# Weight chunks of a mixture-of-experts layer loaded in runs of four instead of two

## The chip, the cores and the metric

The kernel runs on one core of a Trainium2 chip. The metric is the device time of one execution in microseconds (us). All arithmetic is in float32, with float32r (a reduced form) for one scatter product.

## The reference

One layer of a streaming encoder for 256 prompt rows and 64 sample rows of width 1024. First a mixer: RMS norm, one input projection, sliding-window attention with sinks, a short convolution, an output projection and the residual. Then a mixture of experts, in which nearly all of the weight bytes lie:

```
logits = hn @ w_router + b_router                # 32 experts
top 4 per row, gates = softmax of the four logits
for each expert e, on the rows that chose it:
    g, u = split(x @ w_gu[e] + b_gu[e])          # w_gu[e]: 1024 x 2048
    g = min(g, 7);  u = clip(u, -7, 7)
    y = ((u + 1) * g * sigmoid(1.702 * g)) @ w_down[e] + b_down[e]   # 1024 x 1024
h += gate * y, put back to its rows
```

w_gu is 32 x 8 MB and w_down is 32 x 4 MB, 384 MB in all (MB is 2^20 bytes here, KB 2^10), and each expert's weights are read once.

## The kernel before

**Tiling.** 32 experts are worked in 16 pairs. An expert's weights are 12 chunks of 1 MB, each 8 KB on each of 128 partitions: chunks 0 to 7 hold w_gu (one tile k of 128 input features each) and chunks 8 to 11 hold w_down. The two experts of a pair share TensorE: the even one uses 64 columns of the array, the odd one the other 64, and their matmuls run side by side (L854 and L856 for gate and up, L870 and L872 for down). So a step of TensorE needs the same chunk of both experts.

**Order of TensorE's work.** `pair(j)` (L933) does the eight steps k = 0 to 7 of pair j's gate and up, and then the four down steps m = 0 to 3 of pair j - 1. Between the steps stand smaller pieces: after k = 1, 3 and 5 the scatter of pair j - 2 back to its rows (L896, two half tiles each time), after k = 3 and 5 a gather of the rows of pair j + 1 (L787), and after m = 0 the turn of pair j's gate and up results by transposes (L881) and of the one-hot marks (L888). `gate_up` (L849) and `down` (L863) wait for their two chunks (`landed`, L845) and add 1 to `chunk_used` for each chunk when its last matmul is done. IN_USE (L316) lists all 384 chunks in this order, even and odd in turn; `used_up_to(e, c)` is a chunk's place in it.

**The ring.** Chunks land in a ring of 16 slots of 1 MB (L109 to L124). Three chunks have rooms of their own (EARLY_AT, LATE_AT, PIECES_AT); the other 381 go round the ring in the order of ORDER, chunk n in slot (n + 1) mod 16. LOADS (L339) says which neighbours in ORDER come by one DMA: from n = 24 (EARLY) on, two chunks of one expert at a time, 2 MB; the first 24 and the last 36 (FINE) singly. For that ORDER takes two chunks of the even expert, then the same two of the odd one. In DRAM the weights are read so that a partition holds neighbouring rows: 16 KB a partition for two chunks (`gu_dram`, `dn_dram`, L311 and L312).

**Issue.** SyncE issues every load, in order, from one queue (L462 to L464). Before each load it waits until `chunk_used` shows that TensorE is done with what lay in all of the load's slots 16 places earlier in ORDER; a load of several chunks waits for the last of these. The chunks of the first ring turn are issued while the mixer still runs, as its weights leave their rooms (L437 to L456).

**Which row is where.** Since a partition holds neighbouring rows of the weights, the features of x and of the hidden rows are picked with the same stride: `tile_features` (L376) for the gather's columns of hn, `features` (L370) for the columns of gu_sb that the transposes take, and the biases b_guT and the norm's gain g2 are loaded in that order (L443, L527).

Of the kernel before, what the change touches and what calls it, by code (L numbers as in the profile page):

```python
# [15 lines left out]
P = 128  # L16
# [13 lines left out]
def hybrid_layer_kernel(nc, x_prompt, x_sample, cache_k, cache_v, state_conv, norm1_g, w_in, q_norm_g,  # L30
# [15 lines left out]
    FF = w_down.shape[2]  # L46
    KT = D // P
    FT = FF // P
# [12 lines left out]
    FLAT = 2 * FF  # L61
    GUC, DNC = KT, FT * D // FLAT
    CH = GUC + DNC
    FPC = FLAT // D
    RING = 16
# [5 lines left out]
    with ctx:  # L71
# [111 lines left out]
        g2 = sb("g2", [P, KT])  # L183
        b_guT = sb("b_guT", [P, NE, 2 * FT])
# [123 lines left out]

        ADDED_LATE = 2 * NT * (PAIRS - 2) - 2 * NT

        gu_dram = w_gu.rearrange("l e (m p a) f -> (l e) m p (a f)", a=2, p=P)  # L311
        dn_dram = w_down.rearrange("l e (m p a) n -> (l e) m p (a n)", a=2 * FPC, p=P)  # L312

        IN_USE, ORDER = [], []  # L316
        for j in range(PAIRS + 1):
            for pair, chunks in ((j, range(GUC)), (j - 1, range(GUC, CH))):
                if 0 <= pair < PAIRS:
                    IN_USE += [(2 * pair + s, c) for c in chunks for s in range(2)]  # L320
                    ORDER += [(2 * pair + s, c + a) for c in chunks[::2] for s in range(2) for a in range(2)]
        ALL = len(IN_USE)

        EARLY, FINE = 3 * GUC, 4 * GUC + 4
        ORDER[:EARLY] = IN_USE[:EARLY]
        ORDER[ALL - FINE:] = IN_USE[ALL - FINE:]
        EARLY_AT, LATE_AT, PIECES_AT = (1, CH - 1), (NE - 2, 0), (NE - 4, 0)
        for at in (EARLY_AT, LATE_AT, PIECES_AT):
            ORDER.remove(at)
        RINGED = len(ORDER)  # L330
# [2 lines left out]
        def slot_of(n):  # L333
            return (n + 1) % RING
# [3 lines left out]

        LOADS, n = [], 0  # L339
        while n < RINGED - 2:  # L340
            e, c = ORDER[n]
            two = (EARLY <= n < RINGED + 1 - FINE and c % 2 == 0 and ORDER[n + 1] == (e, c + 1)
                   and slot_of(n) < RING - 1)
            LOADS.append((n, 1 + two))
            n += 1 + two

        def quarters(chunk):
            return [chunk[:, n * 512:(n + 1) * 512] for n in range(FLAT // 512)]
# [14 lines left out]
        def key_window(c):  # L363
# [3 lines left out]
            first = max(0, c - WIN // CHUNK)  # L367
            return (first % 2) * CHUNK, (c + 1 - first) * CHUNK

        def features(part, f):  # L370
            m, a = f // (2 * FPC), f % (2 * FPC)
            first = part * FF + m * 2 * FPC * P + a
            return slice(first, first + 2 * FPC * (P - 1) + 1, 2 * FPC)


        def tile_features(k):  # L376
            first = k // 2 * 2 * P + k % 2
            return slice(first, first + 2 * P - 1, 2)

        def most_rows(eng):  # L380
            eng.wait_ge(counts_ready, 2)
# [26 lines left out]
        @block.sync  # L408
        def _(sp):
            def rows_of(e, c, many):  # L410
                src = gu_dram[e, c // 2] if c < GUC else dn_dram[e, (c - GUC) // 2]
                return src[:, c % 2 * FLAT:(c % 2 + many) * FLAT]

            def load(e, c, many, slot):
                sp.dma_start(ring[:, slot:slot + many, :].rearrange("p a n -> p (a n)"),
# [21 lines left out]
            for n in range(RING - 1):  # L437
                slot = slot_of(n)
                if slot == FREE_SLOTS:
                    sp.wait_ge(v_done, 1)  # L440
                if slot == QKV_SLOTS:

                    for q in range(2 * FF // (4 * P)):  # L443
                        sp.dma_start(b_guT[:, :, 4 * q:4 * q + 4],
                                     b_gu[0].rearrange("e (q p a) -> q p e a", p=P, a=4)[q]).then_inc(bias_in, 16)
                    sp.wait_ge(bch_done, 3 * CT)
                if slot == BCH_SLOTS:
                    sp.wait_ge(att_mixed, NCH)
                    sp.wait_ge(conv_mixed, CT)
                    sp.dma_start(early_chunk[:, :], rows_of(*EARLY_AT, 1)).then_inc(early_in, 16)  # L450
                if BCH_SLOTS <= slot < BCH_SLOTS + MIX // 2 - 1:
                    sp.wait_ge(wo_used, slot - BCH_SLOTS + 1)
                if slot == BCH_SLOTS + MIX // 2 - 1:
                    sp.wait_ge(out_done, 2 * NT)
                    sp.wait_ge(u_kept, 2)
                load(*ORDER[n], 1, slot)  # L456
# [46 lines left out]
        @block.gpsimd  # L503
        def _(pool):
            pool.memset(ident[:, :], 0.0).then_inc(zeroed, 1)
            pool.memset(ones[:, :], 1.0).then_inc(zeroed, 1)
            pool.wait_ge(zeroed, 2)
            pool.affine_select(out=ident[:, :], in_=ident[:, :], compare_op=ALU.not_equal, fill=1.0,
                               base=0, pattern=[[-1, P]], channel_multiplier=1).then_inc(consts, 1)

            pool.affine_select(out=before[:, :], in_=ones[:, :], compare_op=ALU.is_gt, fill=0.0,
                               base=0, pattern=[[1, P]], channel_multiplier=-1).then_inc(consts, 1)
            pool.iota(row_ids[:, :], pattern=[[1, CAP]], base=1, channel_multiplier=0,
                      allow_small_or_imprecise_dtypes=True).then_inc(consts, 1)
            pool.wait_ge(consts, 3)
            pool.memset(hn[DEC:P, NT - 1, :], 0.0).then_inc(hn_padded, 1)


            roll = WIN - DEC
            rows_of = lambda a: a[0, 0].rearrange("t h d -> t (h d)")  # L520
            pool.wait_ge(ck_in, 16)
            pool.dma_start(rows_of(new_k_sample)[0:roll, :], ck_nat[DEC:WIN, :]).then_inc(kv_stored, 16)
            pool.wait_ge(cv_in, 16)
            pool.dma_start(rows_of(new_v_sample)[0:roll, :], cv_nat[DEC:WIN, :]).then_inc(kv_stored, 16)
            pool.wait_ge(v_ready, 2)
            pool.dma_start(w_rt[:, :, :], w_router.rearrange("l (k p) e -> p (l k) e", p=P)).then_inc(router_in, 16)
            pool.dma_start(g2[:, :].rearrange("p (m a) -> p m a", a=2),  # L527
                           norm2_g.rearrange("l (m p a) -> p (l m) a", a=2, p=P)).then_inc(router_in, 16)
            pool.dma_start(b_rt[:, :], b_router.to_broadcast([P, NE])).then_inc(router_in, 16)
            pool.dma_start(rows_of(new_v_prompt), v_nat[:, 1, :]).then_inc(kv_stored, 16)  # L530
            pool.dma_start(rows_of(new_v_sample)[roll:WIN, :], v_nat[0:DEC, 2, :]).then_inc(kv_stored, 16)
            pool.wait_ge(k_out_ready, 2)
            pool.dma_start(rows_of(new_k_prompt), k_out[:, 0, :]).then_inc(kv_stored, 16)
            pool.dma_start(rows_of(new_k_sample)[roll:WIN, :], k_out[0:DEC, 1, :]).then_inc(kv_stored, 16)
            pool.wait_ge(chunk_used, used_up_to(*PIECES_AT))
            pool.dma_start(b_dn[:, :], b_down[0]).then_inc(b_down_in, 16)
# [779 lines left out]
        def _(dve):  # L1316
# [309 lines left out]
            for j in range(PAIRS):  # L1626
                if 1 <= j < PAIRS - 1:
                    dve.wait_ge(gathered, 2 * (j + 1))
                    mark(2 * j + 2).then_inc(oh_ready, 1)
                if j == 0:  # L1630
                    finish_routing()
                if j == 1:
                    dve.wait_ge(bias_in, 4 * 16)
                    gate_and_up(1, gu_banks(0), 0)
                if j >= 1:
                    if j >= 2:
                        dve.wait_ge(chunk_used, used_up_to(2 * j - 3, CH - 1))
                    hidden(j, j - 1)
                if j >= 2:
                    dve.wait_ge(gate_ready, j - 1)  # L1640
                    dve.wait_ge(scattered, 2 * NT * (j - 2))
                    split_yl(j - 1, Y)
                for u in range(2 * NT):
                    if j >= 2:
                        add_rows(2 * NT * (j - 2), u, u % 2)
                    if u in (3, 5) and j + 1 < PAIRS:
                        if j >= 1:
                            dve.wait_ge(he_ready, j)
                        copy_xT(j + 2, j + 1, (u - 3) // 2)
                if j >= 1:  # L1650
                    if j >= 2:
                        dve.wait_ge(oh_turned, j - 1)
                    mark_gates(j, 2 * j - 2)
                dve.wait_ge(chunk_used, used_up_to(2 * j + 1, GUC - 1))
                if j >= 1:
                    dve.wait_ge(he_ready, j)
                copy_u(gu_banks(j))
                if j >= 1:
                    gate_and_up(j + 1, gu_banks(j), 2 * j)
                    dve.wait_ge(scattered, 2 * NT * (j - 1))  # L1660
                    if j >= 2:
                        dve.wait_ge(yl_ready, j - 1)
                        dve.wait_ge(yh_ready, j - 1)
                    split_ohT(j, ohT)
# [85 lines left out]
```

## Time and profile before

| | us |
|---|---|
| median of 3 runs (lowest to highest) | 1076.94 (1076.07 to 1077.82) |
| the profiled execution's own time | 1075.5 |
| its span in the profile | 1073.6 |
| TensorE matmuls busy | 1029.4 (96%) |
| VectorE busy | 317.7 (30%) |
| ScalarE busy | 95.7 (9%) |
| share of the chain that ended last: TensorE, DMA | 68%, 30% |
| moved by DMA over the span | 420.31 MB (10^6), mean 391 GB/s |
| granted TensorE clock, mean | 0.989 of 2.4 GHz |

The profile shows one execution. Its page sums each engine's busy time, cuts the span into 40 equal slices, follows the chain of work that ended last, and groups instructions by line. Idle time of an engine is put down to what released it. The end of a matmul is modelled, so TensorE's starts are read here rather than its busy share.

### The profile page before, as it was taken

The numbers are of one execution on the slowest core, as the hardware profiler recorded it, in microseconds if no ns is written. First come the engines' busy times: TensorE is split into PE (matmuls) and PEld (weight loads), VectorE is DVE, ScalarE is ACT, GpSimd is POOL, SyncE is SP. The second block draws the span as 40 slices with busy tenths as digits, with TensorE's granted clock in tenths as the row PEclk, the third lists the DMA queues.
The fourth block names the chain that finished last, engine by engine and source line by source line (L and its number), as shares of the span: only waits on it lengthen the run. The fifth ranks groups of instructions, "written<-read, shape, count | busy, mean of one in ns | idle before, by whom it ended". The sixth has DMA issues, their size and how long they took to land.

```text
span 1073.6 us, 11705 instructions
## 1 busy us (share of the span) xinstructions
PE 1029.4 (96%) x5101; PEld 491.1 (46%) x5102; DVE 317.7 (30%) x491; ACT 95.7 (9%) x163; POOL 8.3 (1%) x20
## 2 busy tenths in 40 slices
PE   9999999999999999989898989989898989999997
PEld 7767454444444443435353534434353435334333
DVE  3533121332323232322313231323223132313243
ACT  2222130100000000000001010000000010100001
POOL 1100000000000000000000000000000000000000
PEclk9999999999999999999999999989999999999999
DMA  9950779999999999999999999999999999999996
GB/s 356 312 118 1 258 279 408 427 427 427 426 428 427 429 428 429 429 429 426 429 429 429 429 429 430 428 427 429 428 429 429 429 430 428 427 418 418 422 421 263
DMA packets 58543, 420.31 MB, mean 391 GB/s; under 512 B 23045, under 2 KB 23345, under 8 KB 29969
## 3 DMA queue, kind: packets, MB, share of 16 engines
q1 hardware_dynamic: 55840, 419.32, 94.6%
q0 software_dynamic: 352, 0.55, 0.2%
q8 instruction: 21, 0.34, 0.1%
q10 hardware_dynamic: 2320, 0.03, 0.1%
q14 instruction: 10, 0.07, 0.0%
HBM read 418.29 MB, written 1.58 MB: 391 GB/s over the span
## 4 chain that ended last, share of the span: by engine, by line
PE 68%; DMA 30%; issue 0%; SPq 0%; DVE 0%; ACT 0%; DVEq 0%
PE ps L854 35%; DMA ring<-in_w_gu_dram 28%; PE ps L787 7%; PE ps L870 6%; PE ps L709 5%; PE ps L896 3%; PE ps L727 3%; DMA ring<-in_w_down_dram 2%; PE ps L585 2%; PE ps L856 1%; PE ps L881 1%; PE ps L738 1%; PE ps L900 1%; PE ps L1024 1%; PE ps L611 1%; PE ps L677 0%
## 5 line engine op out<-in xcount | busy, mean ns | idle before, releaser
L854 PE MATMUL ps<-ring,xT 128*64 128x512 f32 x1008 | 457.3, 607 | 31.5 <-DMA ring<-in_w_gu_dram 31.3
L856 PE MATMUL ps<-ring,xT 128*64 128x512 f32 x1024 | 464.7, 607 | 0.0
L854 PEld LDWEIGHTS ps<-ring,xT 128*64 128x64 f32 x1008 | 135.6, 139 | 306.4 <-issue 301.9
L870 PE MATMUL ps<-ring,he 128*64 128x512 f32 x480 | 213.5, 594 | 3.4 <-DMA ring<-in_w_down_dram 2.5
L872 PE MATMUL ps<-ring,he 128*64 128x512 f32 x472 | 210.5, 596 | 0.0
L1613 DVE TENSOR_TENSOR x<-ps,x 128x512 f32<-128x512 f32 (+1 forms) x84 | 54.3, 683 | 297.8 <-PE ps L896 271.8
L856 PEld LDWEIGHTS ps<-ring,xT 128*64 128x64 f32 x1024 | 137.6, 139 | 0.0
L870 PEld LDWEIGHTS ps<-ring,he 128*64 128x64 f32 x480 | 63.1, 137 | 133.6 <-issue 133.6
L787 PEld LDWEIGHTS ps<-oh,hn 128*128 128x128 f32 x720 | 89.5, 196 | 8.3 <-issue 6.0
L787 PE MATMUL ps<-oh,hn 128*128 128x128 f32 x720 | 91.5, 282 | 0.0
L1256 ACT COPY gu_sb<-ps 128x1024 f32<-128x1024 f32 x16 | 16.2, 1012 | 607.4 <-PE ps L856 607.4
L872 PEld LDWEIGHTS ps<-ring,he 128*64 128x64 f32 x472 | 62.0, 137 | 0.0
L1564 DVE TENSOR_TENSOR xT<-ps,g 128x512 f32<-128x512 f32 (+2 forms) x35 | 22.5, 646 | 97.8 <-PE ps L787 97.8
L1596 DVE TENSOR_TENSOR xT<-ge,xT 128x1024 f32<-128x1024 f32 x16 | 19.6, 1224 | 94.8 <-PE ps L872 94.8
L1572 DVE COPY gu_sb<-ps 128x1024 f32<-128x1024 f32 x16 | 19.6, 1224 | 81.4 <-PE ps L856 81.4
L881 PEld LDWEIGHTS ps<-ident,gu_sb 128*128 128x128 f32 x256 | 32.1, 210 | 13.0 <-issue 13.0
L896 PE MATMUL ps<-y_hi,ohT 128*128 128x512 f32 x84 | 37.9, 451 | 0.0
L1580 DVE TENSOR_TENSOR ge<-ps,b_guT 128x1024 f32<-128x1024 f32 x16 | 19.6, 1225 | 61.0 <-PE ps L881 61.0
L709 PE MATMUL ps<-xnT,w_chc 128*128 128x320 f32 x128 | 36.5, 438 | 0.0
L881 PE MATMUL ps<-ident,gu_sb 128*128 128x128 f32 x256 | 35.1, 290 | 0.0
L896 PE MATMUL ps<-y_lo,ohT 128*128 128x512 f32 x84 | 33.2, 395 | 0.0
L896 PEld LDWEIGHTS ps<-y_hi,ohT 128*128 128x128 f32 x84 | 15.7, 187 | 38.1 <-issue 36.4
(220 smaller groups left out, 623.4 us busy)
## 6 DMA issues: line engine op xcount, KB each, us to landing
ring<-in_w_gu_dram SPq DMA_DIRECT2D x105, 2048.0 KB, 25.8
ring<-in_w_down_dram SPq DMA_DIRECT2D x53, 2048.0 KB, 27.0
ring<-in_w_gu_dram SPq DMA_DIRECT2D x44, 1024.0 KB, 19.6
ring<-in_w_down_dram SPq DMA_DIRECT2D x19, 1024.0 KB, 27.0
w_chc<-in_w_in_dram SPq DMA_DIRECT2D x1, 4096.0 KB, 20.7
w_qkv<-in_w_in_dram SPq DMA_DIRECT2D x4, 768.0 KB, 9.0
w_b<-in_w_in_dram SPq DMA_DIRECT2D x1, 2048.0 KB, 28.3
w_o<-in_w_out_dram SPq DMA_DIRECT2D x2, 1024.0 KB, 28.2
```

The source lines that it names most:

```text
L585: last = mm(ps[:, QK_BANK[i], t0:t1], w_qkv[:, k, cols], xnT[:, k, t0:t1], start=(k == 0 and t0 == 0), stop=(k == KT - 1), skip_group_chec ...
L709: last = mm(ps[:, BCH_BANK[part], 0:TOK], w[:, k, col:col + P], xnT[:, k, :], start=(k == 0), stop=(k == KT - 1))
L727: last = mm(ps[0:n, OUT_BANK[t][half], :], mixT[:, j, t0:t0 + n], w_o[:, j, half * HALF:(half + 1) * HALF], start=(j == 0), stop=(j == MIX ...
L787: last = mm(out[:, k, 0:experts * CAP], hn[:, t, tile_features(k)], marks[:, t, 0:experts, :].rearrange("p s c -> p (s c)"), start=(t == 0 ...
L854: even = mm(gu_banks(j)[0:CAP, n, :], xT[j % 2][:, k, 0:CAP], first[n], start=(k == 0), stop=(k == KT - 1))
L856: odd = mm(gu_banks(j)[CAP:P, n, :], xT[j % 2][:, k, CAP:P], second[n], start=(k == 0), stop=(k == KT - 1))
L870: even = mm(out[0:CAP, half, :], hid[:, f, 0:CAP], first[2 * a + half], start=(f == 0), stop=(f == FT - 1))
L872: odd = mm(out[CAP:P, half, :], hid[:, f, CAP:P], second[2 * a + half], start=(f == 0), stop=(f == FT - 1))
L881: last = nc.tensor.transpose(by_feature(banks)[:, part, f, :], gu_sb[:, features(part, f)], ident[:, :])
L896: last = mm(ps[:, half, :], ohT[:, t * P:(t + 1) * P], y[:, cols], start=(y is y_hi), stop=(y is y_lo and u not in BIASED.get(j, ())), ski ...
L1564: return V.tensor_tensor(xT[j % 2][:, tiles, :], gathered_banks(j)[:, tiles, :], g2[:, tiles].unsqueeze(2).to_broadcast([P, n, 2 * CAP]), ...
L1613: V.tensor_tensor(x[0:m, t, cols], ps[0:m, bank, :], x[0:m, t, cols], ALU.add).then_inc(added, 1)
```

## The change

Chunks are taken in runs of four. The loads in the steady part are 4 MB, 32 KB a partition, and each fills four slots of the same ring of 16. ORDER takes four chunks of the even expert, then the same four of the odd one. w_gu is read as two halves of four tiles, w_down whole with eight rows to a partition. The strides of `tile_features` go from 2 to 4 and those of `features` from 4 to 8, the biases come in two DMAs instead of four, and the gain is read in fours. The single loads at the end start four chunks sooner (FINE is 40, not 36). What TensorE, VectorE and ScalarE compute, in which order and with which waits on each other, stays.

```diff
-        gu_dram = w_gu.rearrange("l e (m p a) f -> (l e) m p (a f)", a=2, p=P)
-        dn_dram = w_down.rearrange("l e (m p a) n -> (l e) m p (a n)", a=2 * FPC, p=P)
+        GU_RUN, DN_RUN = 4, DNC
+        gu_dram = w_gu.rearrange("l e (m p a) f -> (l e) m p (a f)", a=GU_RUN, p=P)
+        dn_dram = w_down.rearrange("l e (p a) n -> (l e) p (a n)", p=P)
...
-            for pair, chunks in ((j, range(GUC)), (j - 1, range(GUC, CH))):
+            for pair, chunks, run in ((j, range(GUC), GU_RUN), (j - 1, range(GUC, CH), DN_RUN)):
                 if 0 <= pair < PAIRS:
                     IN_USE += [(2 * pair + s, c) for c in chunks for s in range(2)]
-                    ORDER += [(2 * pair + s, c + a) for c in chunks[::2] for s in range(2) for a in range(2)]
+                    ORDER += [(2 * pair + s, c + a) for c in chunks[::run] for s in range(2) for a in range(run)]
...
-        EARLY, FINE = 3 * GUC, 4 * GUC + 4
+        EARLY, FINE = 3 * GUC, 5 * GUC
...
         while n < RINGED - 2:
-            e, c = ORDER[n]
-            two = (EARLY <= n < RINGED + 1 - FINE and c % 2 == 0 and ORDER[n + 1] == (e, c + 1)
-                   and slot_of(n) < RING - 1)
-            LOADS.append((n, 1 + two))
-            n += 1 + two
+            (e, c), many = ORDER[n], 1
+            room = min(RING - slot_of(n), RINGED - 2 - n, GU_RUN - c % GU_RUN if c < GUC else CH - c)
+            while n >= EARLY and many < room and ORDER[n + many] == (e, c + many):
+                many += 1
+            LOADS.append((n, many))
+            n += many
...
         def features(part, f):
-            m, a = f // (2 * FPC), f % (2 * FPC)
-            first = part * FF + m * 2 * FPC * P + a
-            return slice(first, first + 2 * FPC * (P - 1) + 1, 2 * FPC)
+            first = part * FF + f
+            return slice(first, first + FT * (P - 1) + 1, FT)
 
         def tile_features(k):
-            first = k // 2 * 2 * P + k % 2
-            return slice(first, first + 2 * P - 1, 2)
+            first = k // GU_RUN * GU_RUN * P + k % GU_RUN
+            return slice(first, first + GU_RUN * (P - 1) + 1, GU_RUN)
...
             def rows_of(e, c, many):
-                src = gu_dram[e, c // 2] if c < GUC else dn_dram[e, (c - GUC) // 2]
-                return src[:, c % 2 * FLAT:(c % 2 + many) * FLAT]
+                src, first = (gu_dram[e, c // GU_RUN], c % GU_RUN) if c < GUC else (dn_dram[e], c - GUC)
+                return src[:, first * FLAT:(first + many) * FLAT]
...
-                    for q in range(2 * FF // (4 * P)):
-                        sp.dma_start(b_guT[:, :, 4 * q:4 * q + 4],
-                                     b_gu[0].rearrange("e (q p a) -> q p e a", p=P, a=4)[q]).then_inc(bias_in, 16)
+                    for q in range(2):
+                        sp.dma_start(b_guT[:, :, FT * q:FT * (q + 1)],
+                                     b_gu[0].rearrange("e (q p a) -> q p e a", p=P, a=FT)[q]).then_inc(bias_in, 16)
...
-            pool.dma_start(g2[:, :].rearrange("p (m a) -> p m a", a=2),
-                           norm2_g.rearrange("l (m p a) -> p (l m) a", a=2, p=P)).then_inc(router_in, 16)
+            pool.dma_start(g2[:, :].rearrange("p (m a) -> p m a", a=GU_RUN),
+                           norm2_g.rearrange("l (m p a) -> p (l m) a", a=GU_RUN, p=P)).then_inc(router_in, 16)
...
-                    dve.wait_ge(bias_in, 4 * 16)
+                    dve.wait_ge(bias_in, 2 * 16)
```

## Rows read from the trace of the kernel before

**Rows 1.** The page: span, and what DMA moved in 40 slices of 26.8 us.

```profile
span 1073.6 us, 11705 instructions
...
GB/s 356 312 118 1 258 279 408 427 427 427 426 428 427 429 428 429 429 429 426 429 429 429 429 429 430 428 427 429 428 429 429 429 430 428 427 418 418 422 421 263
```

**Rows 2.** The page, costliest groups: busy, mean ns | idle before, releaser.

```profile
L854 PE MATMUL ps<-ring,xT 128*64 128x512 f32 x1008 | 457.3, 607 | 31.5 <-DMA ring<-in_w_gu_dram 31.3
```

**Rows 3.** Stretches: us, busy (count) of five engines, clock, DMA share, GB/s.

```profile
165.00:405.00 240.00, 240.00 (x1239) 107.70 (x1238) 69.05 (x96) 14.97 (x14) 0.00 (x0) 1.00 1.01 427
407.94:878.64 470.70, 440.98 (x2168) 199.10 (x2169) 130.56 (x170) 25.46 (x24) 0.00 (x0) 0.98 1.01 428
960.00:1040.00 80.00, 80.00 (x378) 31.35 (x374) 24.46 (x33) 5.25 (x5) 0.00 (x0) 1.00 1.01 421
```

**Rows 4.** TensorE in order of time, pair 4: start, duration in us.

```profile
352.09 0.59 PE L854 MATMUL ps<-ring,xT 128*64 128x512 f32 x1
...
367.20 0.50 PE L896 MATMUL ps<-y_hi,ohT 128*128 128x512 f32 x1
...
371.16 0.64 PE L854 MATMUL ps<-ring,xT 128*64 128x512 f32 x1
...
389.04 0.59 PE L870 MATMUL ps<-ring,he 128*64 128x512 f32 x1
...
404.96 0.59 PE L870 MATMUL ps<-ring,he 128*64 128x512 f32 x1
```

**Rows 5.** The same view: first matmuls of pairs 7, 8, 10, with waits.

```profile
525.41 0.61 PE L854 MATMUL ps<-ring,xT 128*64 128x512 f32 x1 [2.70 <-DMA ring<-in_w_gu_dram]
...
584.14 0.61 PE L854 MATMUL ps<-ring,xT 128*64 128x512 f32 x1 [2.70 <-DMA ring<-in_w_gu_dram]
...
702.44 1.09 PE L854 MATMUL ps<-ring,xT 128*64 128x512 f32 x1 [3.54 <-DMA ring<-in_w_gu_dram]
```

**Rows 6.** Stretches: steps k = 0 and 1 of these pairs.

```profile
525.41:532.43 7.02, 7.02 (x33) 2.62 (x33) 1.10 (x1) 0.00 (x0) 0.00 (x0) 1.00 0.99 420
584.14:592.85 8.71, 8.71 (x32) 3.10 (x32) 1.09 (x1) 0.00 (x0) 0.00 (x0) 0.80 0.99 423
702.44:712.35 9.91, 9.91 (x32) 3.12 (x32) 0.25 (x1) 0.00 (x0) 0.00 (x0) 0.70 1.01 432
```

**Rows 7.** The chain's first DMA; a DMA row (us to landing); SyncE's queue.

```profile
0.79 3.52 DMA x<-in_x_prompt_dram
...
out_dram<-x SPq DMA_DIRECT2D x1, 512.0 KB, 3.4
...
592.92 0.33 SPq L415 DMA_DIRECT2D ring<-in_w_down_dram  x1
```

**Rows 8.** TensorE in order of time, the ring's second turn.

```profile
193.09 0.59 PE L854 MATMUL ps<-ring,xT 128*64 128x512 f32 x1
...
222.26 0.64 PE L854 MATMUL ps<-ring,xT 128*64 128x512 f32 x1
...
229.18 0.59 PE L870 MATMUL ps<-ring,he 128*64 128x512 f32 x1
...
245.51 0.59 PE L854 MATMUL ps<-ring,xT 128*64 128x512 f32 x1
```

**Rows 9.** The same view, from pair 14 to the last down steps.

```profile
934.97 0.61 PE L854 MATMUL ps<-b_dn_room,xT 128*64 128x512 f32 x1 [0.29 <-DMA ring<-in_w_gu_dram]
...
959.36 0.64 PE L854 MATMUL ps<-ring,xT 128*64 128x512 f32 x1
...
1048.21 0.61 PE L870 MATMUL ps<-ring,he_last 128*64 128x512 f32 x1 [1.32 <-DMA ring<-in_w_down_dram]
```

**Rows 10.** Groups by shape, weight loads of strided columns: busy, mean ns.

```profile
L787 PEld LDWEIGHTS ps<-oh,hn 128*128 128x128 f32 x720 | 89.5, 196 | 8.3 <-issue 6.0 <-DVE oh L1499 0.3
...
L881 PEld LDWEIGHTS ps<-ident,gu_sb 128*128 128x128 f32 x256 | 32.1, 210 | 13.0 <-issue 13.0
...
L556 PEld LDWEIGHTS ps<-ident,hn 128*128 128x128 f32 x16 | 1.9, 190 | 0.3 <-DVE hn L1337 0.3
```

More of the change, by code:

```diff
@@ L327, in hybrid_layer_kernel @@
         EARLY_AT, LATE_AT, PIECES_AT = (1, CH - 1), (NE - 2, 0), (NE - 4, 0)
+        assert sorted(ORDER) == sorted(IN_USE)
         for at in (EARLY_AT, LATE_AT, PIECES_AT):
```

## The prediction

> **What bounds the kernel now.** I read the slices first: from 188 us to 939 us DMA moves 426 to 430 GB/s in every slice, though TensorE is called busy 96% of the span [rows 1]. The stretches say the same: 427 GB/s up to 405 us, 428 after it, a DMA share of 1.01 [rows 3]. A pair needs 24 chunks, 25.17 million bytes, and 25.17 / 0.428 = 58.8 us; pair 7 starts at 525.41 and pair 8 at 584.14, 58.73 us apart [rows 5]. So DMA sets the pace. TensorE's own pace is read where it waits for nothing. In pair 4 [rows 4] steps k = 0 to 3 with the scatter between them take 367.20 - 352.09 = 15.11 us; scatter and gather after k = 3 take 3.96 (to 371.16); k = 4 to 7 with theirs 17.88 (to 389.04); the four down steps with the turns 16.5 (to 404.96 + 0.59). That is 53.4 us a pair against 58.73, and the difference is spent waiting, nearly all before k = 0: 2.70 us, once 3.54 [rows 5], 31.3 us in all [rows 2]. Up to 405 us it lived off the chunks that had been loaded ahead. The wait has a second price. After it k = 0 and 1 took 7.02 us at clock 1.00, or 8.71 at a mean clock of 0.80, or 9.91 at 0.70 [rows 6]: the clock falls from 2.4 to 1.2 GHz for a part of them, which costs 1.7 us and, after the one longer wait, 2.9. Today that is free, since DMA is the bound and never stops.
>
> **What keeps DMA from stopping, and what the change does to it.** A load is issued when TensorE has left all of its slots; SyncE follows at once (592.92, the step ended at 592.85) [rows 6, 7]. Before, an even and an odd load together are 4 slots, a quarter of the ring: while TensorE works in one quarter, DMA has up to three queued. After, they are 8 slots, half of the ring. A step needs both experts' chunks, so k = 0 can start only when 8 MB have landed, and none of these slots is free again until k = 3 is done. The ring becomes two halves: TensorE in one, DMA in the other. Three groups of 8 chunks make a pair: A (k 0 to 3), B (k 4 to 7), C (down). The group after next goes into the half that a group leaves.
>
> Two durations are not in the trace and are bounded. (1) D, the landing of 8 MB by 32 KB pieces. Now it is 58.73 / 3 = 19.58 us. With 8 KB pieces the rate is 421 GB/s, with 16 KB 428 [rows 3]: on each of 16 DMA engines 311.3 and 612.5 ns a piece, a fixed 10 ns each, so 32 KB would take 1215 ns, 431.5 GB/s, D = 19.4 (an estimate). Bounds: 421 GB/s (19.9) if long pieces don't help, and 434 (19.3) by the extreme slices, 418 and 430. I take 19.4. (2) H, what passes between the end of TensorE's last step in a half and its first in it again, beyond D. The first 512 KB load took 3.52 us alone; at 428 GB/s its bytes take 1.2, which leaves 2.3; a 512 KB store leaves 2.2 [rows 7]. Bounds: 1 us, if issue overlaps the end of the transfer before it, and 3.5, the whole of the row. I take 2.3.
>
> *A rule.* The row says 2.3 us. The Trainium skill, "DMA: Bandwidth & Descriptors", section "Anatomy of one DMA", puts the fixed part of a DMA at about 2.0 us, mostly the receipt of the last bytes; with it H would be 0.3 less, and the time some 3 us less. Its section "Where 436 GB/s comes from" gives the SBUF ports 435 GB/s, so no packet size could bring D under 19.3 here. [...]
>
> **The sum for a pair**, with A's start at 0. A ends at 15.1 + c, c being the clock's price. Scatter and gather follow, so B may start at 19.1 + c; B landed at D = 19.4. B ends at 19.1 + c + 17.9. Only then is the next A's load issued, and DMA's queue has run empty by then: C landed at 2D = 38.8, or 15.1 + c + H + D, whichever is later. The next A lands at 37.0 + c + H + D = 37.0 + c + 2.3 + 19.4 = 58.7 + c. For DMA to stay the bound (3D = 58.2), c + H would have to be under 1.8. What c is follows from the wait before A: C runs to 37.0 + c + 16.5, so the wait is 5.2 us with c = 2.9, and with c = 0 it is still 3.4. Both are at or above the waits that gave 1.7 to 2.9 [rows 5, 6]; the nearest row, 3.54 us, gave 2.9, and I take that. Period 61.6 us against 58.73.
>
> **The start.** The first 24 chunks come as before. The third four of pair 1 go when its slots are left at 193.09, and seven down chunks behind them, so all have landed by about 222. Experts 4 and 5 (pair 2, A) wait for k = 6 and k = 7 of pair 1: k = 6 starts at 222.26 and k = 7 ends at 229.18 [rows 8], so these are issued at 225.7 and 229.2 and have landed at 225.7 + 2.3 + 9.7 = 237.7 and 247.4. Pair 2 starts there, 1.9 us after its 245.51 [rows 8]. Its B is issued at 242.1 and 245.5 (down m = 2 and 3 of pair 0) and lands at 266.8; B ends at 284.7; pair 3 starts at 284.7 + 2.3 + 19.4 = 306.4. Counted back from the start of pair 7, DMA's pace of today would put it at 525.41 - 4 x 58.73 = 290.5: the lead that DMA builds today, 16 us, is not built, since a full ring can now hold only the half in use and one more.
>
> **The middle and the end.** Pairs 3 to 13: 306.4 + 10 x 61.6 = 922.4. Today pair 13 starts at 584.14 + 5 x 58.9 = 878.6 (the end of the second stretch, [rows 3]). From there C ends 37.0 + 2.9 + 16.5 = 56.4 later and pair 14 starts without a wait, as the odd split of the loads around the piece chunk lets its first seven chunks go sooner. From 934.97 to 959.36 pair 14 takes 24.4 us, 2.1 of them idle, so 22.3; from 959.36 to the end 114.2, of which 1.3 is a wait that goes [rows 9], since TensorE is now behind DMA. Sum 56.4 + 22.3 + 112.9 = 191.6, against 1073.6 - 878.6 = 195.0. Span: 922.4 + 191.6 = 1114.0, +40.4. The profiled execution lay 1.9 over its span and 1.4 under the median, so 1077 + 40 gives 1117; with the clock's price a little under 2.9 in some pairs, I say 1116.
>
> **Edits at no cost.** Half as many bias packets: DMA is idle in the fourth slice (1 GB/s) [rows 1], behind which they end, and if that cover went, they could only gain. Strides: weight loads of columns 2, 4 and 8 apart take 196, 210 and 190 ns [rows 10], so neither gather nor turn should change; if the gather went the way from 196 to 210, 24 of them on the path are at most 0.3 us a pair, +4 us. FINE: the four chunks more that come singly near the end come at 421 instead of 428 GB/s, 0.2 us in all, where TensorE is the bound.
>
> **Rivals.**
> 1. *Halves bind, but the clock falls less.* With c = 1.7 the period is 60.4, 12 us less: 1104. With c = 0, as in pair 7 after 2.70 us [rows 5, 6], it is 58.7, the last part 190.5, and 306.4 + 587 + 190.5 - 1073.6 = +10: 1087. Against it: the waits would be longer than any that gave 0.
> 2. *DMA keeps the pace.* Place: the handover after k = 7. It decides once c + H is under 1.8, when the next A's bytes start before C's are in. Then a pair is 58.2, and if the start isn't held up either, 318 chunks at 0.023 us less each give -7, at 434 GB/s -11: 1066 to 1070. For it: the rates in [rows 3]. Against it: H alone is over 1.8, and the start loses time even with H = 1.
> 3. *The larger pieces don't do what they say.* D = 19.6 to 19.9, the halves bind all the same: period +0.2 to +0.5, 1118 to 1122. For it: 16 KB pieces gave only 7 GB/s over 8 KB.
>
> **Chances.** Forecast 0.55 (own range 1108 to 1128), rival 1 0.27 (0.15 of it near 1104), rival 2 with its middle ground 0.08, rival 3 0.10. Upward the bounds are H = 3.5 (+13) and the gather (+4): 1134. I leave out half of rival 2 below and little above: 1084 to 1133. Within 0.2% (2.2 us; finer than this a measurement can't tell) 0.03, faster 0.05, slower 0.92.
>
> **What would show it.** The starts of pairs 61 to 62 us apart from pair 3 on, pair 3 near 306, a wait of some 5 us before each k = 0 with k = 0 and 1 taking 9 to 10 us; L854's idle time over 50 us; DMA's share about 0.95 (58.2 / 61.6), near 409 GB/s in the middle; TensorE hardly waiting from pair 14 on. Starts 58.2 apart and a share of 1.0 would prove rival 2; starts of 58.7 and waits over 3 us at full clock, rival 1. Wrong altogether I'd be if a half's slots were refilled before its last step is done.

## The result, and the profile after

| | before | after |
|---|---|---|
| median, us | 1077.1 (4 runs) | 1203.6 (4 runs, 1202.5 to 1203.9) |
| ratio | | 1.118, 95% interval 1.116 to 1.119 |
| span in the profile | 1073.6 | 1201.9 |
| wait of gate and up on DMA | 31.3 | 71.3 |

The change costs 126.5 us. I had forecast 39 us (1116, range 1084 to 1133): the sign is right, the size is not.

The page of the changed kernel (span; GB/s in slices of 30 us; the costliest groups with busy time, mean ns, idle before them):

```profile
span 1201.9 us, 11625 instructions
...
GB/s 357 327 18 14 314 342 305 319 383 435 318 411 323 417 316 435 315 401 420 330 419 314 434 320 433 309 427 382 348 418 334 417 316 422 381 412 384 420 422 177
...
L858 PE MATMUL ps<-ring,xT 128*64 128x512 f32 x1008 | 470.4, 621 | 71.3 <-DMA ring<-in_w_gu_dram 71.3
...
L791 PEld LDWEIGHTS ps<-oh,hn 128*128 128x128 f32 x720 | 170.9, 328 | 7.2 <-issue 5.8 <-DVE oh L1503 0.3
L791 PE MATMUL ps<-oh,hn 128*128 128x128 f32 x720 | 171.7, 395 | 0.0
```

Slices that held 426 to 430 GB/s [rows 1] now swing between 305 and 435. The loads reach the higher rate while they run, but DMA stands still in between. And the gather (L787 before, L791 now) has weight loads of 328 ns where it had 196 [rows 10]: a group that was no part of the sum.

TensorE in order of time, pair 4 to the start of pair 5, as in [rows 4]: A begins, A's last step has ended, B begins, C begins, the next A begins.

```profile
398.25 1.08 PE L858 MATMUL ps<-ring,xT 128*64 128x512 f32 x1 [5.81 <-DMA ring<-in_w_gu_dram]
...
416.13 0.50 PE L900 MATMUL ps<-y_hi,ohT 128*128 128x512 f32 x1
...
422.73 0.64 PE L858 MATMUL ps<-ring,xT 128*64 128x512 f32 x1
...
443.26 0.59 PE L874 MATMUL ps<-ring,he 128*64 128x512 f32 x1
...
466.08 1.09 PE L858 MATMUL ps<-ring,xT 128*64 128x512 f32 x1 [6.45 <-DMA ring<-in_w_gu_dram]
```

SyncE's queue in the same pair (four loads from here on, the next A's first):

```profile
443.46 17.30 SPq L419 DMA_DIRECT2D ring<-in_w_gu_dram  x4
```

| us | forecast | pair 4 after |
|---|---|---|
| A, with the clock's price | 18.0 | 17.9 |
| scatter and gather before B | 4.0 | 6.6 |
| B | 17.9 | 20.5 |
| end of B to the next A (H + D) | 21.7 | 22.8 |
| period | 61.6 | 67.8 |

The chain is the one forecast: the next A's load goes out 0.2 us after B's end, and TensorE starts again 22.6 us later (forecast 21.7). Each of the two stretches that hold a gather is 2.6 longer. Over the stretch of pairs 3 to 12 (busy times of the five engines, clock, DMA share, GB/s), and over k = 0 and 1 of pairs 3 and 4:

```profile
332.09:1001.54 669.45, 609.39 (x2710) 296.58 (x2711) 162.75 (x210) 31.81 (x30) 0.00 (x0) 0.95 0.89 375
...
332.09:340.78 8.69, 8.69 (x33) 2.77 (x33) 0.00 (x0) 0.00 (x0) 0.00 (x0) 0.80 1.00 434
398.25:407.98 9.73, 9.73 (x32) 3.13 (x32) 0.00 (x0) 0.00 (x0) 0.00 (x0) 0.72 1.00 431
```

The same view in steps of 4 us, in pair 9 (B ends at 710.7):

```profile
700.00:704.00 4.00, 4.00 (x19) 3.88 (x20) 0.02 (x1) 0.00 (x0) 0.00 (x0) 1.00 1.16 500
704.00:708.00 4.00, 4.00 (x20) 1.29 (x18) 1.69 (x3) 0.00 (x0) 0.00 (x0) 1.00 0.09 33
708.00:712.00 4.00, 4.00 (x20) 1.29 (x18) 1.04 (x1) 1.01 (x1) 0.00 (x0) 1.00 0.22 57
712.00:716.00 4.00, 4.00 (x27) 2.33 (x24) 0.74 (x2) 0.00 (x0) 0.00 (x0) 1.00 0.86 336
```

DMA has nothing to do for some 7 us, while TensorE finishes B in the half that the next A is to fill: the queue had run empty, as the sum said. (In stretches this short the rate swings with where the 32 KB pieces fall; the gap is what is read.) The mean period is (1001.54 - 332.09) / 10 = 66.9 us. Less two gathers at 2.66 it is 61.6, the forecast; that the two agree so closely is in part luck, as two terms were off in opposite directions (below). DMA's share is 0.89, and the clock falls at each A from pair 3 to pair 13 as in [rows 6].

### The profile page after: what moved, and what is told of

Same layout as the page of the kernel before. It is cut to its first block, busy times and chain, and to the rows that moved or that the text cites. A ratio compares the mean times of both kernels' runs of the same rounds, so it can differ in the third digit from the quotient of the medians.

```text
span 1201.9 us, 11625 instructions
## 1 busy us (share of the span) xinstructions
PE 1122.8 (93%) x5101; PEld 572.9 (48%) x5102; DVE 317.7 (26%) x491; ACT 95.7 (8%) x163; POOL 8.3 (1%) x20
## 4 chain that ended last, share of the span: by engine, by line
PE 77%; DMA 22%; SPq 0%; issue 0%; POOL 0%; DVE 0%; POOLq 0%
PE ps L858 39%; DMA ring<-in_w_gu_dram 22%; PE ps L791 15%; PE ps L713 4%; PE ps L874 4%; PE ps L900 4%; PE ps L731 2%; PE ps L589 2%; PE ps L860 1%; PE ps L885 1%; PE ps L552 1%; PE ps L742 1%; PE ps L904 1%; PE ps L1028 1%; PE ps L615 0%; PE ps L681 0%
## 5 line engine op out<-in xcount | busy, mean ns | idle before, releaser
L858 PE MATMUL ps<-ring,xT 128*64 128x512 f32 x1008 | 470.4, 621 | 71.3 <-DMA ring<-in_w_gu_dram 71.3
L860 PE MATMUL ps<-ring,xT 128*64 128x512 f32 x1024 | 477.6, 621 | 0.0
L858 PEld LDWEIGHTS ps<-ring,xT 128*64 128x64 f32 x1008 | 138.5, 143 | 359.0 <-issue 354.7
L791 PEld LDWEIGHTS ps<-oh,hn 128*128 128x128 f32 x720 | 170.9, 328 | 7.2 <-issue 5.8
L791 PE MATMUL ps<-oh,hn 128*128 128x128 f32 x720 | 171.7, 395 | 0.0
L860 PEld LDWEIGHTS ps<-ring,xT 128*64 128x64 f32 x1024 | 140.6, 143 | 0.0
L874 PEld LDWEIGHTS ps<-ring,he 128*64 128x64 f32 x480 | 64.4, 137 | 130.6 <-issue 130.6
L1568 DVE TENSOR_TENSOR xT<-ps,g 128x512 f32<-128x512 f32 (+2 forms) x35 | 22.5, 646 | 180.3 <-PE ps L791 180.3
L876 PEld LDWEIGHTS ps<-ring,he 128*64 128x64 f32 x472 | 63.3, 137 | 0.0
```

The costliest lines, as they stand in the source:

```text
L791: last = mm(out[:, k, 0:experts * CAP], hn[:, t, tile_features(k)], marks[:, t, 0:experts, :].rearrange("p s c -> p (s c)"), start=(t == 0 ...
L858: even = mm(gu_banks(j)[0:CAP, n, :], xT[j % 2][:, k, 0:CAP], first[n], start=(k == 0), stop=(k == KT - 1))
L860: odd = mm(gu_banks(j)[CAP:P, n, :], xT[j % 2][:, k, CAP:P], second[n], start=(k == 0), stop=(k == KT - 1))
L874: even = mm(out[0:CAP, half, :], hid[:, f, 0:CAP], first[2 * a + half], start=(f == 0), stop=(f == FT - 1))
L876: odd = mm(out[CAP:P, half, :], hid[:, f, CAP:P], second[2 * a + half], start=(f == 0), stop=(f == FT - 1))
L1568: return V.tensor_tensor(xT[j % 2][:, tiles, :], gathered_banks(j)[:, tiles, :], g2[:, tiles].unsqueeze(2).to_broadcast([P, n, 2 * CAP]), ...
```

## The experiments

Two things were to be told apart: what the gather's stride costs, and what the ring in halves costs; then which property of the load makes the halves. The kernel before ran again beside them, with medians of 1076.4 us (15 runs) and 1076.3 us (27 runs); ratios and losses below are against these.

**gather_contiguous.** The changed kernel, its gather on neighbouring columns:

```diff
-                A(hn[0:n, t, :], x[0:n, t, :], ACT.Copy, scale=st[0:n, 2, t:t + 1]).then_inc(hn_ready, 1)
+                A(hn[0:n, t, :].rearrange("q (m a p) -> q m a p", a=GU_RUN, p=P),
+                  x[0:n, t, :].rearrange("q (m p a) -> q m a p", a=GU_RUN, p=P), ACT.Copy,
+                  scale=st[0:n, 2, t:t + 1]).then_inc(hn_ready, 1)
...
-            first = k // GU_RUN * GU_RUN * P + k % GU_RUN
-            return slice(first, first + GU_RUN * (P - 1) + 1, GU_RUN)
+            return slice(k * P, (k + 1) * P)
```

> The changed kernel with one thing undone: ScalarE writes the normed rows hn in the order of the tiles, so that each gather takes 128 neighbouring columns instead of columns 4 apart. Ring, loads and weight layout are those of the change. Theory A (two costs that add: the gather's weight loads went from 196 to 328 ns, 24 of them from 2.98 to 5.64 us, twice in each of 16 pairs on the path that frees the ring's slots, 85 us; and the ring in two halves, which I had forecast alone at +40): the gather's cost goes and 1203.6 - 85 = 1118 us is left, pairs 61.5 us apart. Rival B (the loads of 32 KB a partition themselves are slow, or disturb TensorE's reads): the gathers get shorter but the time stays above 1180. Rival C (the gather is all of the loss, the halves cost nothing): 1077 or under.

Measured 1121.9 us, ratio 1.042 (1.040 to 1.043). Its gather's weight loads, and the starts of pairs 12 and 13:

```profile
L790 PEld LDWEIGHTS ps<-oh,hn 128*128 128x128 f32 x720 | 85.1, 192 | 8.4 <-issue 6.0 <-DVE oh L1504 0.3
```

```profile
869.30 1.09 PE L857 MATMUL ps<-ring,xT 128*64 128x512 f32 x1 [4.50 <-DMA ring<-in_w_gu_dram]
...
930.74 1.09 PE L857 MATMUL ps<-ring,xT 128*64 128x512 f32 x1 [4.59 <-DMA ring<-in_w_gu_dram]
```

61.4 us apart here; from pair 3 to pair 13 the starts are 60.5 to 64.2 apart, 62.0 on average. Theory A holds, B and C fall. 81.7 us of the loss go with the stride. What is left, +45.5, is what the prediction had summed as +39.

With the gather short again, TensorE waits in places that the sum had at nothing: before the down steps of most pairs, and before B in pairs 4, 6 and 9 (1.5, 2.2 and 3.4 us).

```profile
L873 PE MATMUL ps<-ring,he 128*64 128x512 f32 x480 | 216.7, 605 | 18.3 <-DMA ring<-in_w_down_dram 18.3
```

**slow_gather_old_ring.** The kernel before with the gather's stride alone:

```diff
-            first = k // 2 * 2 * P + k % 2
-            return slice(first, first + 2 * P - 1, 2)
+            first = k // 4 * 4 * P + k % 4
+            return slice(first, first + 4 * (P - 1) + 1, 4)
```

> The kernel before with the gather's columns 4 apart instead of 2 (so the gathered features are not those that belong to the weights) and nothing else: loads, ring and layout as before. Theory A: 5.3 us more a pair on TensorE make 53.4 + 5.3 = 58.7 us a pair, just DMA's 58.73, so the loss is the start (pair 2 at 262 instead of 245.5), the lead that is not used up, and the end: about 1110 us, with hardly a wait on DMA left. Rival B (the gather costs nothing where DMA bounds): 1077. Rival C (the gather is all of the loss in the changed kernel): 1200.

Measured 1106.9 us, ratio 1.029 (1.027 to 1.030). Its gather is slow as in the changed kernel:

```profile
L787 PEld LDWEIGHTS ps<-oh,hn 128*128 128x128 f32 x720 | 170.9, 328 | 7.1 <-issue 5.8 <-DVE oh L1499 0.3
```

No wait of TensorE on the ring's DMA is listed in it any more. So the same slow gather costs 30.5 us beside the old ring, where it first uses up the time spent waiting, and 81.7 beside the halved one, where all of it is on the path.

**clock_kept.** gather_contiguous, and work for TensorE ahead of each wait:

```diff
+                if 2 <= j < PAIRS - 2:
+                    keep_busy(4, 20)
                 for k in range(GUC):
```

> The kernel with contiguous gathers, and 20 small matmuls of the identity (some 4.5 us) into a free bank ahead of the wait before k = 0, in pairs 2 to 13. They fill most of a wait of 5 us. Theory A (k = 0 and 1 run at 1.2 GHz for a part after the wait, and with the half-ring this is on the path): k = 0 and 1 take 7.1 us in every pair instead of 8.7 to 9.9, and 10 to 11 pairs win some 2.3 us each, 25 us against gather_contiguous, so about 1094. Rival (the clock's price is hidden by a wait that follows): the same time as gather_contiguous.

Measured 1103.1 us (4 runs, 1100.7 to 1107.6), 18.8 less than gather_contiguous. In pair 9 the small matmuls stand before k = 0, and k = 0 and 1 (the stretch is theirs) run at full clock:

```profile
665.63 4.73 PE L551 MATMUL ps<-ident 128*128 128x128 f32 x40
```

```profile
670.36:677.31 6.95, 6.95 (x33) 2.14 (x33) 0.00 (x0) 0.00 (x0) 0.00 (x0) 1.00 0.91 391
```

So the clock's price is real and on the path; the rival falls. The 18.8 is a lower bound: k = 0 starts as the filling ends, so the filling itself may have held it up a little. It fits what the trace of gather_contiguous shows: there k = 0 and 1 of pairs 2 to 13 take 20.7 us more in sum than at 7.02 each, 1.7 a pair. I had expected 25, at 2.3 a pair.

**big_group_small_loads.** gather_contiguous, in the same order, two chunks a load:

```diff
-            while n >= EARLY and many < room and ORDER[n + many] == (e, c + many):
+            while n >= EARLY and many < min(2, room) and ORDER[n + many] == (e, c + many):
```

> The kernel with contiguous gathers, in the changed kernel's order (four chunks of the even expert, then four of the odd one), but by loads of 2 MB, two slots each. This tells the order of eight from what one load holds: after two steps the first two slots are free and their load goes out, so only six of eight chunks are left to issue when the half is done. Theory A (what costs is that DMA's queue runs empty while a load waits for four slots): DMA has 4.9 us of work more when the half ends, more than the handover of some 3 us, so it hardly stops; between 1076 and 1085 us against 1121.9 for gather_contiguous. Rival (a group of 8 MB that both experts need is by itself too large for a ring of 16, whatever the loads): 1105 or over.

Measured 1078.7 us, ratio 1.0023 (1.0014 to 1.0032). DMA in it, up to 405 us and in the middle:

```profile
165.00:405.00 240.00, 232.24 (x1208) 105.22 (x1208) 67.69 (x94) 14.97 (x14) 0.00 (x0) 1.00 1.00 424
407.00:880.00 473.00, 441.72 (x2184) 193.77 (x2182) 130.16 (x168) 25.47 (x24) 0.00 (x0) 0.97 1.01 428
```

In the middle DMA never stops. Groups of 8 MB are no harm there in a ring of 16 MB; a load that takes its four slots only when all four are free is. That one property is 43.2 of the 45.5 us, the clock's price included. The other 2.3 us go with the order and seem to lie in the start (424 GB/s against 427 [rows 3]): the ninth slice of the page, 26.8 us long, moved 391 GB/s against 427 [rows 1], some 2 us of standing still, and 425 in old_ring_new_layout (next), which has the old order.

**old_ring_new_layout.** gather_contiguous with the order and loads of before:

```diff
-                    ORDER += [(2 * pair + s, c + a) for c in chunks[::run] for s in range(2) for a in range(run)]
+                    ORDER += [(2 * pair + s, c + a) for c in chunks[::2] for s in range(2) for a in range(2)]
```

> The kernel with contiguous gathers and the changed kernel's layout in DRAM and on chip (features by fours and eights), in the order and by the loads of before: two chunks of the even expert, two of the odd one, 2 MB each. Theory A (the layout costs nothing but the gather's stride): 1077, the time of before. Rival (runs of 16 KB at a pitch of 32 KB, transposes of columns 8 apart, or the biases cost something): 1082 or over.

Measured 1076.5 us, ratio 1.0002 (0.9992 to 1.0011). The layout in DRAM, the transposes 8 apart and the biases in two DMAs cost nothing.

**odd_even_odd.** gather_contiguous with loads of 2, 4 and 2 MB in each group of eight:

```diff
-                    ORDER += [(2 * pair + s, c + a) for c in chunks[::run] for s in range(2) for a in range(run)]
+                    ORDER += [(2 * pair + s, c + a) for c in chunks[::run]
+                              for s, part in ((1, (0, 1)), (0, range(run)), (1, (2, 3))) for a in part]
```

> The kernel with contiguous gathers, and in each group of eight chunks the ring's order is two of the odd expert, four of the even one, two of the odd one. Loads of 2 MB, 4 MB, 2 MB: the first two slots come free after two steps and are refilled while TensorE is still in the half, so DMA keeps a load queued; k = 0 waits for 6 chunks instead of 8. Theory A (what is left of the loss is DMA standing still while a whole half is refilled, plus the lead that is not built): DMA never stops, half of the bytes come at 434 instead of 428 GB/s, pairs 58.3 us apart, 1070 to 1074. Rival B (large pieces cost by themselves): no better than 1100.

Measured 1075.3 us (11 runs), ratio 0.9990 (0.9981 to 0.9999). Its middle, and the starts of pairs 6 and 7:

```profile
407.00:880.00 473.00, 441.12 (x2197) 193.60 (x2192) 130.19 (x168) 25.45 (x24) 0.00 (x0) 0.98 1.00 430
```

```profile
474.05 0.62 PE L858 MATMUL ps<-ring,xT 128*64 128x512 f32 x1 [3.09 <-DMA ring<-in_w_gu_dram]
...
532.58 0.61 PE L858 MATMUL ps<-ring,xT 128*64 128x512 f32 x1 [3.12 <-DMA ring<-in_w_gu_dram]
```

58.5 us apart against 58.73 [rows 5]: half of the bytes in pieces of 32 KB bring 430 for 428 GB/s; DMA's share is 1.00, so with smaller loads between them the loads of four slots stop it no more. That is all that pieces of 32 KB in half of the bytes are worth, and theory A had put it a little too high (1070 to 1074). The order of eight with 2 MB loads gave 428, so the rate goes with the pieces and not with the order.

**odd_even_odd_late.** The same with chunks 24 to 38 single:

```diff
-        EARLY, FINE = 3 * GUC, 5 * GUC
+        EARLY, FINE = 5 * GUC, 5 * GUC
...
-            while n >= EARLY and many < room and ORDER[n + many] == (e, c + many):
+            while n >= EARLY - 1 and many < room and ORDER[n + many] == (e, c + many):
```

> odd_even_odd, with chunks 24 to 38 of the ring loaded singly as well, in order of use, before the larger loads begin. In odd_even_odd DMA moved 396 GB/s in the ninth slice, where before had 427: a load of three or four slots waits there for a step of pair 1. Theory A (these stops lose 1.9 us, single pieces 0.3): 1.5 us better than odd_even_odd, 1073.8. Rival (the lead at the start is worth nothing to a DMA-bound kernel): the same as odd_even_odd.

Measured 1074.9 us, ratio 0.9987 (0.9978 to 0.9996) to the kernel before. It is the fastest of all, but its 0.5 us over odd_even_odd are within both intervals, so the expectation is neither shown nor refuted. The stops that it was to remove mostly stayed: its ninth slice moved 402 GB/s, against 396 in odd_even_odd and 427 before.

**stride_3_and_1 and stride_8_and_2.** The kernel before with other strides in `tile_features` (3, then 8) and in `features` (1, then 2). They ran once each, in 1083.5 and 1112.0 us beside 1075.7 of the kernel before; only their durations of single instructions are used. The first of the two:

```diff
-            first = k // 2 * 2 * P + k % 2
-            return slice(first, first + 2 * P - 1, 2)
+            first = 3 * k
+            return slice(first, first + 3 * (P - 1) + 1, 3)
```

> The kernel before with two strides changed (the features then don't match the weights): the gather takes columns 3 apart, the turn of the gate and up results columns 1 apart. Of the gather's weight loads 196 ns is known at 2, 328 at 4, 192 at 1. Theory A (the step costs once it passes 16 bytes a column, or reaches it: a threshold): 196 or so at 3. Rival (the cost grows with the step): about 260 at 3. For the turn, 210 ns at 4 and 192 at 8 are known; with no stride near 140, as the transposes of x at L746.

> The kernel before with two strides changed (the features then don't match the weights): the gather takes columns 8 apart, the turn columns 2 apart. Theory A (a threshold at 4 columns, as with every element in another 16 bytes): the gather's weight loads stay at 328 ns at 8. Rival 1 (it grows with the step): over 500. Rival 2 (a pattern special to 4): back to about 200, as the turn's loads went from 210 at 4 to 192 at 8. The turn at 2: between 140 and 210.

Groups by shape of stride_3_and_1, then of stride_8_and_2 (mean ns is the last number before the second bar):

```profile
L786 PEld LDWEIGHTS ps<-oh,hn 128*128 128x128 f32 x720 | 130.2, 261 | 7.2 <-issue 5.8 <-DVE oh L1498 0.3
L880 PEld LDWEIGHTS ps<-ident,gu_sb 128*128 128x128 f32 x256 | 27.7, 140 | 13.0 <-issue 13.0
```

```profile
L786 PEld LDWEIGHTS ps<-oh,hn 128*128 128x128 f32 x720 | 174.1, 334 | 7.3 <-issue 5.8 <-DVE oh L1498 0.3
L880 PEld LDWEIGHTS ps<-ident,gu_sb 128*128 128x128 f32 x256 | 31.9, 209 | 13.0 <-issue 13.0
```

| columns apart (4 bytes each) | 1 | 2 | 3 | 4 | 8 |
|---|---|---|---|---|---|
| gather's weight load, ns | 192 | 196 | 261 | 328 | 334 |
| transpose's weight load, ns | 140 | 209 | - | 210 | 192 |

No theory was right throughout: at 3 the rival's 260 came true (261), at 8 theory A's 328 (334). The gather's load is flat up to 2, grows at 3 and 4 and stays there. It grows up to 16 bytes a column and no further. The Trainium skill, "SBUF — State Buffer", section "Specifications (TRN2)", has lines of 16 bytes in SBUF of which two elements must be taken each for full speed. For the gather the runs agree: at 2 apart a line gives two elements and the load is nearly as fast as at 1 (196 ns against 192), at 4 and at 8 it gives one and the load takes 1.7 times as long. Another sentence of that page of the Trainium skill, in its section "Door 1: The DMA port swizzle (why `[64,N]` ≈ `[32,N]`)", that one can stride for free up to 4 fp32, they don't bear out (328 ns at 4), and the transposes follow neither: theirs rises from 140 to 209 ns at 2 already. Why they differ is not shown.

The trace of the kernel before held one more row, of transposes that read neighbouring columns:

```profile
L746 PEld LDWEIGHTS ps<-ident,x 128*128 128x128 f32 x16 | 1.7, 140 | 0.9 <-issue 0.8
```

Beside the 210 ns of L881 [rows 10] it said that a stride can cost half as much again.

## Why the prediction was wrong, point by point

- **What bounds the kernel**: right. DMA did; in slow_gather_old_ring, at 58.6 us a pair, TensorE just takes its place.
- **The step that failed** is "Strides: weight loads of columns 2, 4 and 8 apart take 196, 210 and 190 ns [rows 10], so neither gather nor turn should change", with a bound of 0.3 us a pair, +4 us. Measured: 2.66 us for each gather, 5.3 us a pair, 81.7 us in all. The rows at 4 and 8 are transposes and the one at 2 is a matmul, and I put them in one series. The table above shows two series: from 2 apart on, the transpose's stays near 200 where the gather's rises from 196 to 328. The bound was also counted for one gather, 24 loads, where a pair has two of them on the path, 48. The rows themselves held a sign that they differ: L881's 256 weight loads are one for each of 16 pairs' 16 transposes, while a gather of 12 matmuls shows as 24 (L787 x24 in the trace), two loads each. The nearest row of the right kind, an f32 matmul 4 apart, was not in the trace, and the bound should then have been wide.
- **Its place was right, its size was not.** The prediction counted the gather's loads on the path, and they are: the halves make TensorE's whole time from A's start to B's end a part of the period, so each us of it counts in full. With the old ring the gather costs 30.5 us, with the halves 81.7.
- **The ring in halves**: right in mechanism and nearly in size. gather_contiguous is the changed kernel without the stride: forecast 1116, measured 1121.9; pair 3 forecast at 306.4, there at 310.7; period 61.6, there 62.0 on average ((930.74 - 310.70) / 10). The period is that near by luck. Over pairs 3 to 12 the clock cost 1.7 us a pair and not 2.9; from B's end to the next A it took 22.6 and not 21.7; and waits before B, which the sum had at nothing, took 0.7. The waits for C show the same handover: its chunks land 15.1 + c + H + D after A's start, the sum's own term, and with H at 3.1 that is behind B's end.
- **H and D**: end of B to the next A, forecast 21.7, was 22.1 to 24.0 in the changed kernel, mean 22.5. With D = 19.4 that makes H 3.1, not 2.3, inside its bounds (1 to 3.5). D alone is in no trace, so the split is an estimate. The 2.0 us of the Trainium skill ("DMA: Bandwidth & Descriptors", section "Anatomy of one DMA — SWDGE (gpsimd) path") that the prediction set beside H would have been further off; that section is on DMAs issued from GpSimd, and these loads are issued by SyncE.
- **The clock's price**: forecast 2.9 in each pair; k = 0 and 1 took 8.5 to 10.0 us in the changed kernel, 1.5 to 3.0 over 7.02, 2.3 on average. It did not grow with the wait: after the longest, 7.58 us before pair 3, it was 1.7. Keeping the clock up gave back 18.8 us.
- **The larger pieces**: forecast 431.5 GB/s for 32 KB. odd_even_odd moved 430 with half of its bytes so; the other half at 428 leaves about 432. (The bound "by the extreme slices, 418 and 430" comes out at 436 GB/s by the prediction's own formula, not 434; nothing hung on it.)
- **The start**: pair 2 forecast at 247.4, and 265.83 in the changed kernel; the slow gathers before it are the difference, since in gather_contiguous it is 249.1.
- **The rivals**: 2 and 3 fell. Rival 1, a smaller price of the clock, was half right: its 1.7 us is what gather_contiguous shows, but the time did not come down to 1104, as H and the waits before B took back what the clock left. None of them was the gather; it stood only among the upward bounds, at 4 us.

How the 126.5 us divide, each from two kernels that differ in one thing (the gather's contiguous columns brought slower copies on ScalarE with them, some 1 us for each of three row tiles, which old_ring_new_layout shows to cost nothing): 1203.6 to 1121.9 the stride, 1121.9 to 1078.7 the load of four slots, 1078.7 to 1076.5 the order; the layout's part is under 1. The parts depend on the way taken: undo the ring first, and it is worth 96.7 (1203.6 to 1106.9) and the stride 30.5.

## What to carry to other kernels

A load that waits for several slots turns a ring into so many fewer, larger ones: count how many loads can be queued while the consumer works in the slots of one, and put the smallest load first in a group, as its slots come free first. Where a buffer goes from quarters to halves, the consumer's time joins the period and slack that hid other costs is gone, so every small edit made beside it is to be priced anew. Take the price of a changed access pattern only from a row of the same operation; a transpose says nothing of a matmul.

## What the runs showed of the hardware

- Here a float32 matmul's weight load of 128 columns took 192, 196, 261, 328 and 334 ns at strides of 4, 8, 12, 16 and 32 bytes; a transpose's 140, 209, 210 and 192 at 4, 8, 16 and 32.
- DMA from DRAM moved 421, 428 and about 432 GB/s in pieces of 8, 16 and 32 KB. From 16 to 32 KB the size is worth 1%. The 432 is worked out from the 430 of a kernel with half of its bytes in such pieces.
- ScalarE's copy of 1024 columns, read 4 apart and written in a row, took 2147 ns in gather_contiguous, and 1148 when read in a row (in the kernel before):

```profile
L1224 ACT ACTIVATE hn<-x,st 128x1024 f32<-128x1024 f32 x2 | 4.3, 2147 | 0.5 <-DVE st L1474 0.5
```

It stands once for each row tile, and bought the gather's contiguous columns.
